# The order of ten items in the attention stage of the sample group, and what moves with it

## The reference

```
o_cmp, o_sel = nsa_cmp_sel(q, full_cmp, full_sel, q_pos, pe, w1, w2)   # 2048 cached tokens + 1 new
kv_w = concatenate([win_buf, kv_win], axis=1)                          # 512 rows + the new one
o_win = window_attn_dense(q, kv_w, q_pos, k_pos)                       # distance 0 to 511
o_b = gates[0] * o_cmp + gates[1] * o_sel + gates[2] * o_win
```

## Time and profile before

| | |
|---|---|
| median of 3 runs | 2890.97 us (2890.41 to 2892.94) |
| the profiled execution | 2890.97 us, of which the span is 2889.2 us |
| TensorE matmuls busy | 2792.6 us, 97% of the span |
| VectorE, ScalarE, POOL busy | 1193.1, 625.1, 1008.0 us |
| chain that ended last | PE 79%, issue 8%, DVE 6%, ACT 3%, POOL 2%, DMA 1% |
| DMA | 185.46 MB, mean 64 GB/s |
| POOL's DMA queue q0 | 16.78 MB, 1.6% of 16 engines' span |

### The profile page before, as it was taken

One profiled execution on the slowest core, in us unless ns is written; L12 is line 12 of the kernel. 1 busy time (PEld: TensorE's weight loads), 2 busy tenths in 40 slices (PEclk: granted clock), 3 DMA queues, 4 the chain that ended last, 5 costly groups with the idle time before them and its releaser, 6 DMA issues.

```text
span 2889.2 us, 49270 instructions
## 1 busy us (share of the span) xinstructions
PE 2792.6 (97%) x21195; PEld 2662.0 (92%) x21195; DVE 1193.1 (41%) x1244; ACT 625.1 (22%) x1092; POOL 1008.0 (35%) x484
## 2 busy tenths in 40 slices
PE   7999989999898999999999999999999999999998
PEld 7999878876776799999999999999999999999998
DVE  6111283345543325344443445226335434443345
ACT  4100044556665311100110002210120110001102
POOL 6332100100002464444444445443555344444340
PEclk9999999999999999999999999999999999999999
DMA  5111243210203621111111111311211111111111
GB/s 179 50 46 41 83 143 102 84 41 2 89 2 117 239 61 46 44 51 44 44 45 50 44 51 44 118 52 37 96 37 52 52 44 44 50 44 44 50 51 59
DMA packets 204235, 185.46 MB, mean 64 GB/s; under 512 B 8013, under 2 KB 185426, under 8 KB 202362
## 3 DMA queue, kind: packets, MB, share of 16 engines
q1 hardware_dynamic: 193290, 160.28, 17.9%
q0 software_dynamic: 4608, 16.78, 1.6%
q10 hardware_dynamic: 6192, 6.29, 0.8%
HBM read 162.41 MB, written 25.09 MB: 65 GB/s over the span
## 4 chain that ended last, share of the span: by engine, by line
PE 79%; issue 8%; DVE 6%; ACT 3%; POOL 2%; DMA 1%; SPq 0%; POOLq 0%; DVEq 0%; ACTq 0%
PE psum L266 50%; PE psum L476 6%; PE psum L298 5%; PE psum L1505 4%; PE psum L1892 2%; PE psum L286 2%; DVE xlo L338 2%; PE psum L1866 1%; POOL whl L237 1%; PE psum L1489 1%; PE psum L1829 1%; POOL whl L240 1%; DVE nmax L1996 1%; DMA wraw<-in_w_in_ab 1%; PE psum L313 1%
## 5 line engine op out<-in xcount | busy, mean ns | idle before, releaser
L266 PE MATMUL psum<-xhi,whl 128*128 128x344 f32 x4656 | 863.8, 320 | 1.1 <-ACT vCs L692 0.6
L237 POOL TENSOR_TENSOR whl<-wraw,zeroc 128x1024 fp32r<-128x1024 f32 x186 | 372.9, 2005 | 1154.0 <-PE psum L266 814.6
L266 PEld LDWEIGHTS psum<-xhi,whl 128*128 128x128 f32 x4656 | 756.1, 188 | 2.0 <-issue 1.7
L240 POOL TENSOR_TENSOR whl<-wraw,whl 128x1024 fp32r<-128x1024 f32 x186 | 501.6, 2697 | 14.6
L266 PE MATMUL psum<-xlo,whl 128*128 128x344 f32 x2328 | 494.0, 320 | 0.0
L266 PE MATMUL psum<-ahi,whl 128*128 128x344 f32 x2304 | 427.5, 319 | 0.2
L266 PEld LDWEIGHTS psum<-xlo,whl 128*128 128x128 f32 x2328 | 394.0, 189 | 0.0
L266 PEld LDWEIGHTS psum<-ahi,whl 128*128 128x128 f32 x2304 | 373.1, 188 | 4.4 <-DVE ftmp L558 3.7
L545 DVE CAST ahi<-frel 128x1032 fp32r<-128x1032 f32 x64 | 171.2, 2675 | 475.5 <-ACT frel L522 475.1
L520 ACT ACTIVATE frel<-psum 128x1032 f32<-128x1032 f32 x64 | 66.2, 1034 | 1234.2 <-PE psum L266 1189.9
L558 DVE TENSOR_TENSOR ftmp<-psum,fscale 128x1032 f32<-128x1032 f32 x127 | 156.3, 1231 | 307.7 <-PE psum L266 247.3
(11 more groups left out here) (430 smaller groups left out, 3040.0 us busy)
## 6 DMA issues: line engine op xcount, KB each, us to landing
wraw<-in_w_ffn SPq DMA_DIRECT2D x128, 512.0 KB, 3.8
rows<-in_cache_cmp_kv SPq DMA_DIRECT2D x128, 128.0 KB, 2.5
wraw<-in_w_in_ab SPq DMA_DIRECT2D x26, 512.0 KB, 3.8
hT<-h_spill SPq DMA_DIRECT2D x8, 1032.0 KB, 8.0
wraw<-in_w_in_c SPq DMA_DIRECT2D x16, 512.0 KB, 3.8
h_spill<-hT SPq DMA_DIRECT2D x4, 1032.0 KB, 8.0
h_spill<-hT SPq DMA_DIRECT2D x1, 4128.0 KB, 12.7
wrow<-in_state_win_kv SPq DMA_DIRECT2D x4, 1024.0 KB
```

Source lines behind the costliest of these rows:

```text
L237: pool.tensor_tensor(whl[:, s, 0, :], raw, zeroc[:, 0:1].to_broadcast([P, UNIT]), ALU.add).then_inc(w_hi, 1)
L240: pool.tensor_tensor(whl[:, s, 1, :], raw, whl[:, s, 0, :].bitcast(F32), ALU.subtract).then_inc(w_ready, 1)
L266: last = pe.matmul(psum[:, 3 * bset + c, 0:TC], w, rhs[ah][:, k0 + k, c * TC:(c + 1) * TC], start=(k == 0 and n == 0), stop=(k == kn - 1 a ...
```

## The change

The list of items is reordered: s0 and s1 go first, then w0, then s2. w1 stays where it is. With it, some tiles trade places: the second window buffer `wrow1` and the third key tile `ktb2` lie where the score tile `sc` and three small row tiles lay, and these lie where `wrow1` was. So SP's load of `wrow1` now waits for the last scores of the prompt's attention (`p_qk`) and not for a step of the sample's queries (`p_ea`). s4 now takes the buffer of s1, and s5 that of s0. POOL's first split of the output weights waits for V of s4 and not of s5, since s4 is now the last item in the buffer that lies over it. `dve_selected` starts with the masking of item 0, since item 0 is now a selected one, and two conditions on the item's number follow from that.

```diff
-        wrow = [at("wrow0", R_W + 8192, [P, 2, 4, 256]), at("wrow1", R_H, [P, 2, 4, 256])]
+        wrow = [at("wrow0", R_W + 8192, [P, 2, 4, 256]), at("wrow1", R_G, [P, 2, 4, 256])]
...
-        ktb = [at("ktb0", R_W, [P, 4, 512]), at("ktb1", R_G + 24832, [P, 4, 512]), at("ktb2", R_H, [P, 4, 512])]
-        sc = at("sc", R_G, [P, 2, 512])
+        ktb = [at("ktb0", R_W, [P, 4, 512]), at("ktb1", R_G + 24832, [P, 4, 512]), at("ktb2", R_G, [P, 4, 512])]
+        sc = at("sc", R_H, [P, 2, 512])
...
-        ITEMS = ("w0", "s0", "s1", "s2", "s3", "s4", "w1", "s5", "s6", "s7")
+        ITEMS = ("s0", "s1", "w0", "s2", "s3", "s4", "w1", "s5", "s6", "s7")
...
-        BUFFER = (0, 1, 2, 3, 0, 1, 2, 3)
+        BUFFER = (0, 1, 2, 3, 1, 0, 2, 3)
...
-            order = ["mx0"]
+            order = ["ma0", "mx0"]
...
-            sp.wait_ge(p_ea, step_done(2))
+            sp.wait_ge(p_qk, len(SOFT))
             window_rows(1)
             new_rows(1)
             sp.wait_ge(sP, PE_S[f"V{place('w0')}"])
...
-                    if p >= 2:
-                        act.wait_ge(sP, PE_S[f"PT{p - 2}"])
+                    act.wait_ge(sP, PE_S[f"PT{p - 2}"])
...
-                if n == 0:
+                if p == 0:
                     dve.wait_ge(s_m16, 4)
...
-            pool.wait_ge(sP, PE_S[f"V{place('s5')}"])
+            pool.wait_ge(sP, PE_S[f"V{place('s4')}"])
             pool_split(pool, phases["ab_out"], 1)
```

More of the change, by code:

```diff
@@ L2078, in build @@
         R = NB * HB
-        wrow = [at("wrow0", R_W + 8192, [P, 2, 4, 256]), at("wrow1", R_H, [P, 2, 4, 256])]
+        wrow = [at("wrow0", R_W + 8192, [P, 2, 4, 256]), at("wrow1", R_G, [P, 2, 4, 256])]
         srows = [at(f"srows{x}", off, [P, 4, 1024]) for x, off in
                  enumerate((R_G + 49664, R_W + 16384, R_G + 33280, R_G + 8256))]
-        ktb = [at("ktb0", R_W, [P, 4, 512]), at("ktb1", R_G + 24832, [P, 4, 512]), at("ktb2", R_H, [P, 4, 512])]
-        sc = at("sc", R_G, [P, 2, 512])
+        ktb = [at("ktb0", R_W, [P, 4, 512]), at("ktb1", R_G + 24832, [P, 4, 512]), at("ktb2", R_G, [P, 4, 512])]
+        sc = at("sc", R_H, [P, 2, 512])
         qe = at("qe", R_H + 4096, [R, 16, 64])
-        rowd = at("rowd", R_G + 4096, [2, 5, 32])
-        rown = at("rown", R_G + 4736, [2, 5, 32])
-        rows1 = at("rows1", R_G + 5376, [2, 3, 32])
+        rowd = at("rowd", R_H + 4096, [2, 5, 32])
+        rown = at("rown", R_H + 4736, [2, 5, 32])
+        rows1 = at("rows1", R_H + 5376, [2, 3, 32])
         qm = at("qm", R_H + 8192, [P, NB, R])
```

## The result

The changed kernel takes 2909.32 us (median of 4 runs, 2906.31 to 2912.68), the kernel before in the same comparison 2890.82 us (2890.41 to 2892.94). The ratio is 1.0059, 95% interval 1.0044 to 1.0075: 18.5 us slower, where 10 were forecast, and 1 us above the end of the stated range (2908 us). The profiled execution took 2908.42 us.

What follows compares the result with a forecast made beforehand. TensorE's timeline carries any delay in the sample stage onward, while gathers fill the DMA engines there. 2890.97 us + 9 (w1's late rows) + 1.5 (clock) = 2901.5, stated as 2901 us; range 2892 to 2908 us.

Steps and rivals of the forecast that it cites:

- The late load: Third window load, moved from 785 us to the scores' end: lands 931.5 us, margin 3 us, cost 0.
- the early split: POOL's first output unit split at 974.4 us, not 980.40; nothing waits for it: cost 0, between -0.2 and +0.3 us.
- Gathers s1 and s4: Sample stage: s1 lands at 928.2 us, wanted 934.55; s4 lands at 954.9 us, wanted 956.03; no stall.
- V(w0): Values product of item w0 on TensorE: ends at 950.72 us, and SP then issues w1's windows.
- the clock at the opening: First sample steps: one step with a window item trades places with another; cost 0, within 0.1 us either way.
- the order of service: DMA during the sample stage: each of 16 engines takes requests in order of arrival, giving w1's 9 us delay.
- The windows' start: w1's window loads, ready at 952.1 and 952.8 us, start when s4's gathers are done at 954.6 us.
- The wait: TensorE at w1's third block: waits for the second new row, 9 us, from a spread of 7 to 10.5.
- The row that misled: Profile row, 968.0 to 969.5 us: gathers fill the engines, no q1 packet; taken as evidence for service in order.
- Turns: Rival for w1's windows: engines alternate between q0 and q1, half the time each; 6.4 us late, 2898.6 us; chance 0.18.
- Gathers first: Rival for w1's windows: q1 moves only when q0 is empty; 17 us late, 2909.5 us; chance 0.07.
- The clock behind the stall: TensorE after w1's stall: granted clock falls, work at half speed costs 0.5 to 2.5 us, taken as 1.5.

Runs made afterwards that it cites:

- e1: Kernel before with only the second window buffer's load waiting for the prompt's last scores, against the kernel before: 2896.6 us against 2898.5, ratio 0.9989.
- e3: Old item order with the changed tile places and the late load, against the kernel before: 2899.7 us against 2898.5, ratio 1.0004.
- e11: Changed kernel run a third time without an edit, against the kernel before: 2907.1 us against 2891.7, ratio 1.0057.
- e9: Changed kernel with w0 as second item, the old gather buffers and first split after s5's values product, against the kernel before: 2891.1 us against 2891.7, ratio 0.9995.
- e4: Changed kernel run again without an edit, against the kernel before: 2903.8 us against 2898.5, ratio 1.0012.
- e8: Kernel before run again unchanged, against the kernel before: 2898.2 us against 2898.7, ratio 0.9999.
- e5: Changed kernel with s5's gathers also waiting for w0's values product, against the kernel before: 2915.5 us against 2898.7, ratio 1.0056.
- e7: Kernel before with s4's gather waiting for s1's values product, so eight gathers go in a row, against the kernel before: 2904.6 us against 2898.7, ratio 1.0020.
- e6: Changed kernel with the old gather buffers and the first split again after s5's values product, against the kernel before: 2907.3 us against 2898.7, ratio 1.0028.
- e12: Changed kernel with window rows loaded in 4 KB pieces instead of 1 KB, against the kernel before: 2906.4 us against 2899.8, ratio 1.0023.
- e2: Changed item order, buffers and split with the old tile places and early window load, against the kernel before: 2908.3 us against 2898.5, ratio 1.0034.
- e10: Changed kernel with s5's gathers held until w1's last new row landed, s6's and s7's until later scores, against the kernel before: 2903.0 us against 2891.7, ratio 1.0042.

## Why the prediction was right in its direction and short in its size

- *Kept.* The late load, the places of the tiles and the early split cost nothing that e1 and e3 can tell from no change, and nothing waits for the split. Gathers s1 and s4 were in time. V(w0) ended at 951.35 us in e11, where 950.72 was worked out, and SP followed at once.
- *Unforeseen, but not the change's: the clock at the opening.* In e11 items 0 and 1 run at half clock until about 936 us, and item 1 starts 8.06 us after item 0, where it was 7.20 (934.55 - 927.35); with the step behind it 1.6 us in all. I had put 0 within 0.1 us, and that isn't refuted: e9 on the same chip does not have the 1.6 us, but e4, the same kernel as e11, starts item 1 7.20 us after item 0, and e8 and e1, with the old order, 8.06 and 8.07 us. It differs between executions with either order.
- *Wrong: the order of service.* The step that failed reads "as if each of the 16 engines took requests in the order in which they come". The windows' start still agrees with it: they were to begin at 954.6 us, when s4's gathers were served, and did by 955. But in place of order for all that followed, e11 and e5 show turns by packet (340 and 343 packets, 344 and 342). The gathers of s6 and s7, issued from 957 us, after the windows, then count against them as well, and three quarters of the time is theirs. The wait was 14.79 + 0.49 us for 9 forecast, and 13.13 us in e5.
- *The row that misled.* That no packet of q1 moved in 968.0 to 969.5 us I read as order for the whole transfer. It is a late start: in e11 q1 shows none until 954.5 us, 3.1 us after its issue, and then gets its turns. In the kernel before, too, the weights did not wait until the gathers were done: in 969.5 to 970 us q1 moved 24 packets beside 47 of q0. That q1 first waited for the gathers issued before it would explain the length of the late start, but no run tests this. The same row had been held against "Turns", which was the right mechanism with the wrong share: half the time each gave 6.4 us. The Trainium skill (DMA: Bandwidth & Descriptors, "Queues, rings and completion order") says that an engine goes round-robin between its queue rows and drains a packet of descriptors from one before it switches. The equal counts agree with such turns (whether the profile counts these packets or single descriptors isn't shown), and the measured share of 25% for q1 replaces the 40% that I had estimated from its figures. "Gathers first" gave 17 us, near the measured 15.3, by a rule that the 25% refutes: slow turns and last place end alike when the other queue is never empty.
- *The clock behind the stall.* Item 6 to item 7 takes 6.63 us in e11 for 5.38, of it 0.15 a longer wait: 1.1 us, for 1.5 forecast.

The sum for e11 against the earlier trace rows, from stage start to output product: 1.6 + 14.9 (15.28 less the 0.34 idle in the earlier trace rows) + 1.1 = 17.6 us, and the rows give (1002.35 - 926.38) - (985.59 - 927.35) = 17.7. Against e9 on the same chip the span is 2903.7 - 2886.1 = 17.6 us longer. Without the opening the change's own part is 14.9 + 1.1 = 16.0 us; by medians the difference on D is 15.4 us.

**The first profile is another sum.** In it the hold (7.8 us at item 4) stood in for the stall, and the opening (10.5 us by item 1) came on top. The opening is made of shorter holds, each beside POOL's gathers: 0.8 us of it are there before the first gather, 3.6 us come beside those of s0, 2.0 us beside those of s1 and s2, 4.1 us beside those of s3, part of that at half clock. Two of the holds in rows, VectorE beside s0's four gathers in the kernel before and in the changed kernel, then ScalarE beside s3's four in the changed kernel and in e7:

```profile
874.56 0.69 DVE L2037 TENSOR_TENSOR otmp<-psum,wgt 128x512 f32<-128x512 f32 x1 [0.63 <-PE psum L1892]
877.41 0.69 DVE L2037 TENSOR_TENSOR otmp<-psum,wgt 128x512 f32<-128x512 f32 x1 [2.35 <-remote]
```

```profile
942.30 1.08 ACT L2508 ACTIVATE ktb<-psum 128x512 f32<-128x512 f32 x2 [5.99 <-remote]
937.94 1.09 ACT L2508 ACTIVATE ktb<-psum 128x512 f32<-128x512 f32 x2 [5.90 <-remote]
```

e7 has the old order, and the first row's hold is in every profile of B, C and E, with either order (2.21 to 2.24 us idle), and in none of D (0.61 to 0.63). So the opening isn't the change's. The trace of the kernel before has none of these holds, the first profile of the changed kernel has all of them. Where the profiles show them (B, C, E), the kernel before has medians of 2898.5 to 2899.8 us, and 2891.7 us on D, where they don't; in the first comparison it had 2890.8. By an estimate from these medians some 7.5 of the 18.5 us can come from that and 11 are left for the change; since the chips of the first comparison aren't on record, this stays open. That this profile was slower in the forecast's direction is in part luck: the forecast's own wait was 0.50 us in it.

Nor is it settled why counts are held while gathers are issued in a row. The long hold beside eight in a row came in the profiles of A, B and E, and not on D with the same eight (946.31 to 955.93 us). On C, e5 and e6, with four in a row, have only the short ones, and e7, with eight, agrees with the long one; the changed kernel itself wasn't run there.

None of the versions was faster than the kernel before: e1, e3, e4 and e9 can't be told from it.

## What to carry to other kernels

When a transfer is moved behind a busy queue, count the packets of both and not the bytes: by the equal turns of these runs a load in 1 KB packets gets a quarter of the engines beside gathers of 4 KB, and requests that come after it slow it too. A transfer's margin is used up at one point: w0 in second place cost nothing, in third place a wait of 9 to 15 us, by where the gathers stood (e6, e5, e11). And where the wait that was forecast is missing in a profile, look for a second delay that covers it, and take that away, before the first is called wrong.

## What the runs showed of the hardware that was not expected

- SP went on 6.4 to 6.5 us after the values product that it waited for had ended, 1.8 to 1.9 us after the last of eight gathers that POOL issued in a row (first profile, e4, e12; in e2 the same 6.4 us), and on D at once. Beside four in a row VectorE and ScalarE went on about 1 us after the fourth (first profile, e5 to e8), up to 4.2 us after TensorE had ended, and on D at once.
- Two queues with work moved equally many packets (343 and 340 in e11, 342 and 344 in e5), though one's were 3.7 KB and the other's 1.0 KB, and again (382 and 380 in e10) where the other's were 0.5 KB.
- A queue that was filled behind another's backlog moved nothing for 3.1 us (e11), where an idle one began after 1.3 us (790.71 to 792.0 us, kernel before). It goes the other way too: in e11 POOL's gathers of s1, issued from 918.10 us behind the third window load, moved nothing before 922 us, while q1 moved 0.93 MB.
- Alone on the engines, packets of 4 KB moved 0.82 MB in 2 us (e12), packets of 1 KB 0.73 MB (e4, another chip).
- The same kernel before had medians of 2890.8, 2891.7, 2898.5, 2898.7 and 2899.8 us in five comparisons, so a difference of 0.2% is read only within one of them.
